# Decay products inside blocks of eight tokens as one job, and the units dealt over six jobs

## The reference, cut to what matters

```python
log_f = logaddexp(log(lb), log1p(-lb) + log_sigmoid(f_logit)); k = -expm1(log_f)
bc = cumsum(chunks(log_f), axis=3)                 # inside chunks of 64 tokens
o_inter = einsum('bhtk,bhkv->bhtv', q_ * exp(b_), state)
diff = where(causal, b_[:, :, :, None, :] - b_[:, :, None, :, :], -inf)
attn = einsum('bhtk,bhsk,bhtsk->bhts', q_, k_, exp(diff))
o_intra = einsum('bhts,bhsv->bhtv', attn, v_)
state = state * exp(b_last) + einsum('bhsk,bhsv->bhkv', k_ * exp(b_last - b_), v_)
```

## Time and profile before

| | us |
|---|---|
| median of 3 runs | 1922.56 (1920.65 to 1923.75) |
| the profiled execution | 1921.48, its span 1919.3 |
| TensorE / VectorE / ScalarE busy | 1732.6 / 864.8 / 633.9 |
| granted clock of TensorE, mean | 0.938 |

### The profile page before, as it was taken

The page is one execution under the profiler, slowest core; times in us unless marked ns, Lnnn a source line. Parts: engine busy times, 40 slices in busy tenths (PEclk is TensorE's granted clock), DMA queues, the critical chain, the costliest instruction groups (busy, mean ns, idle before and its releaser), DMA issues.

```text
span 1919.3 us, 31472 instructions
## 1 busy us (share of the span) xinstructions
PE 1732.6 (90%) x12618; PEld 1247.0 (65%) x12618; DVE 864.8 (45%) x1532; ACT 633.9 (33%) x1057; POOL 60.0 (3%) x58
## 2 busy tenths in 40 slices
PE   8999888888889899988878888999999999999997
PEld 7985334334345768543434334699988979998897
DVE  5642122121225644312212122578966556986654
ACT  4422111111114642211101111464537555443753
POOL 0100000000000010000000000100001200000110
PEclk9999889898889989988889889999989999999999
DMA  7659999999997315999999999454522334443222
GB/s 294 240 219 414 421 421 422 421 422 421 422 422 302 122 44 216 416 421 422 421 421 422 421 421 421 175 175 141 190 86 91 104 117 159 149 176 110 88 96 103
DMA packets 73095, 526.41 MB, mean 274 GB/s; under 512 B 8240, under 2 KB 8496, under 8 KB 9264
## 3 DMA queue, kind: packets, MB, share of 16 engines
q1 hardware_dynamic: 73008, 525.18, 68.7%
HBM read 524.10 MB, written 1.05 MB: 274 GB/s over the span
## 4 chain that ended last, share of the span: by engine, by line
PE 52%; DMA 28%; DVE 8%; SPq 6%; ACT 3%; issue 2%; POOL 0%; DVEq 0%; ACTq 0%
PE banks L492 13%; DMA ring<-experts 13%; DMA arena<-experts 12%; PE banks L496 10%; PE banks L498 9%; PE banks L497 9%; SPq L431 6%; PE banks L656 5%; DMA ring<-dense 3%; PE banks L638 3%; PE banks L674 3%; DVE arena L1491 1%; ACT ring_parts L1075 1%; DVE hT L1616 1%; DVE ring_parts L1471 1%
## 5 line engine op out<-in xcount | busy, mean ns | idle before, releaser
L496 PE MATMUL banks<-arena_parts,ring_parts 128*128 128x256 f32 (+1 forms) x1444 | 423.3, 293 | 17.4 <-POOL arena_parts L1404 5.8
L498 PE MATMUL banks<-arena_parts,ring_parts 128*128 128x256 f32 (+1 forms) x1444 | 412.7, 286 | 0.0
L497 PE MATMUL banks<-arena_parts,ring_parts 128*128 128x256 f32 (+1 forms) x1444 | 412.3, 286 | 0.0
L492 PEld LDWEIGHTS banks<-arena 128*128 128x128 f32 (+3 forms) x2704 | 327.7, 193 | 70.6 <-issue 54.3
L492 PE MATMUL banks<-arena 128*128 128x128 f32 (+5 forms) x2704 | 362.8, 289 | 9.2 <-ACT arena L1075 5.2
L656 PE MATMUL banks<-ring,arena 128*32 128x512 f32 x1536 | 235.2, 716 | 104.6 <-DMA ring<-experts 104.5
L1075 ACT ACTIVATE arena<-banks 128x256 f32<-128x256 f32 (+7 forms) x384 | 165.0, 457 | 424.6 <-PE banks L492 164.1
L1471 DVE TENSOR_TENSOR ring_parts<-ring,ring_parts 128x1024 fp32r<-128x1024 f32 x204 | 244.2, 1238 | 120.1 <-ACT ring_parts L1075 118.2
L496 PEld LDWEIGHTS banks<-arena_parts,ring_parts 128*128 128x128 f32 x1444 | 276.3, 191 | 31.9 <-issue 7.4
L497 PEld LDWEIGHTS banks<-arena_parts,ring_parts 128*128 128x128 f32 x1444 | 276.9, 192 | 0.1
L498 PEld LDWEIGHTS banks<-arena_parts,ring_parts 128*128 128x128 f32 x1444 | 276.3, 191 | 0.0
(11 more groups left out here) (214 smaller groups left out, 1613.5 us busy)
## 6 DMA issues: line engine op xcount, KB each, us to landing
ring<-experts SPq DMA_DIRECT2D x192, 1024.0 KB, 26.5
arena<-experts SPq DMA_DIRECT2D x160, 1024.0 KB, 22.0
ring<-dense SPq DMA_DIRECT2D x112, 1024.0 KB, 4.9
at<-experts SPq DMA_DIRECT2D x16, 1024.0 KB, 23.8
x<-experts SPq DMA_DIRECT2D x16, 1024.0 KB, 22.9
consts<-consts_in SPq DMA_DIRECT2D x1, 1414.0 KB, 13.6
vecs<-vecs_in SPq DMA_DIRECT2D x1, 1125.5 KB, 16.0
hT<-h_in SPq DMA_DIRECT2D x2, 544.0 KB, 4.5
```

The costliest lines, as they stand in the source:

```text
L492: return pe.matmul(o, lhsT, rhs, start=(k == 0), stop=(k == n - 1))
L496: pe.matmul(o, lhsT[0], rhs[0], start=(k == 0), stop=False)
L497: pe.matmul(o, lhsT[0], rhs[1], start=False, stop=False)
L498: return pe.matmul(o, lhsT[1], rhs[0], start=False, stop=(k == n - 1))
```

## The change

Spans 8, 4 and 2 and the diagonal become one job, `NEAR`, for all pairs with the key not behind the query inside blocks of eight tokens. The reference token is the fourth of the block for all of them; so both factors are made for all tokens, ScalarE makes two exps for each part (one with scale -1, straight into `b_ke` and `b_qe`), and VectorE multiplies at full width. Exponents of both signs occur now, so the floor under the logarithm, `LN_LEAST`, is raised from 2^-63 to 2^-28. The mask of the new job is the sum of the three spans' masks and the identity, made by three additions of 128x128 in the first mixture of experts. There are six jobs with products (`SPANS`), the new one first, and a seventh entry in `JOBS` without. The units and the rest are dealt over them anew; with `JOBS` the order of `MAKES`, so of the weights in memory, changes. `SPLIT_AT` is gone: one `lower_next` at each of both places in every job.

```diff
--- before.py
+++ after.py
@@ -46,7 +46,7 @@
 LEVELS = (64, 32, 16, 8, 4, 2)
 CHUNK = 64
 PAIRS = 2 * HEADS
-LN_LEAST = 2.0 ** -63
+LN_LEAST = 2.0 ** -28
 CONV_UNITS = 16
@@ -84,17 +84,20 @@
 U_HF, U_HI, U_KC, U_VC, U_KS, U_KW, U_NQ, U_VS, U_VW, U_NZ, U_HZ = 0, 8, 12, 13, 14, 15, 16, 20, 21, 22, 26
 FIRST = [("unit", u) for u in range(U_HI)]
 JOBS = [[("unit", U_HI), ("unit", U_HI + 1)],
-        [("unit", U_KC), ("unit", U_HI + 2)],
-        [("unit", U_VC), ("unit", U_HI + 3)],
-        [("unit", U_KS), ("unit", U_NQ), ("c1", 0)],
-        [("unit", U_NQ + 1), ("c1", 1), ("rot", U_KS), ("rot", U_NQ)],
-        [("unit", U_NQ + 2), ("c1sum", 0), ("c1", 2), ("rot", U_NQ + 1)],
-        [("unit", U_NQ + 3), ("unit", U_KW), ("c1", 3), ("rot", U_NQ + 2)],
-        [("unit", U_VS), ("c1sum", 1), ("rot", U_NQ + 3), ("rot", U_KW)],
+        [("unit", U_KC), ("unit", U_HI + 2), ("unit", U_HI + 3)],
+        [("unit", U_VC), ("unit", U_KS), ("c1", 0), ("unit", U_NQ)],
+        [("c1", 1), ("rot", U_KS), ("unit", U_NQ + 1), ("c1sum", 0), ("c1", 2), ("unit", U_NQ + 2)],
+        [("rot", U_NQ), ("unit", U_KW), ("c1", 3), ("rot", U_NQ + 1), ("unit", U_NQ + 3), ("c1sum", 1)],
+        [("rot", U_KW), ("unit", U_VS), ("rot", U_NQ + 2), ("rot", U_NQ + 3)],
         [("c2", 0), ("c2", 1), ("unit", U_VW), ("crot", 0)]]
 POSITIONS = {2: 0, 3: 1}
-SPLIT_AT = {0: (1, 1), 1: (1, 1), 2: (1, 1), 3: (1, 1), 4: (0, 1), 5: (0, 1), 6: (1, 1), 7: (0, 1)}
+NEAR = 8
+SPANS = (NEAR, 64, 32, 16, P, SEQ)
+MASK_OF = {64: 0, 32: 1, 16: 2, NEAR: 3, P: 6}
 BEFORE_HEADS = [("unit", U_NZ), ("unit", U_HZ)]
 IN_HEADS = [("unit", u) for u in (U_NZ + 1, U_HZ + 1, U_NZ + 2, U_HZ + 2, U_HZ + 3, U_NZ + 3)]
 GATED = {1: (0, 1), 3: (2, 3), 4: (4,), 5: (5,)}
@@ -904,24 +907,24 @@
                 for m in FIRST[6:]:
                     make(*m)
                 t.next(b2["gate_ready"])
-                for job in range(9):
+                for job in range(len(JOBS)):
                     for m in JOBS[job]:
                         make(*m)
+                    if job == len(SPANS):
+                        break
                     for part in range(2):
                         heads = range(4 * part, 4 * part + 4)
                         if job:
-                            pe.wait_ge(b2["lv_at"], 18 * layer + 2 * job - (part == 0 and job < 8))
-                        if job < 8:
-                            t.next(b2["lv_kq"])
-                        keys, queries = (b_ke, b_qe) if job < 8 else (b_k, b_p[:, F_Q:F_Q + HEADS])
+                            pe.wait_ge(b2["lv_at"], 2 * len(SPANS) * layer + 2 * job - (part == 0))
+                        t.next(b2["lv_kq"])
                         for h in heads:
-                            if job == 7:
+                            if SPANS[job] == SEQ:
                                 m = mm(flat[:, 2048 + h * P:2048 + h * P + P], b_ke[:, h, 0:P], b_qe[:, h, P:SEQ], 0, 1)
                                 continue
                             for i in range(2):
                                 at = 2048 + (2 * h + i) * P
-                                m = mm(flat[:, at:at + P], keys[:, h, i * P:i * P + P], queries[:, h, i * P:i * P + P], 0, 1)
+                                m = mm(flat[:, at:at + P], b_ke[:, h, i * P:i * P + P], b_qe[:, h, i * P:i * P + P], 0, 1)
                         m.then_inc(b2["lv_mm"], 1)
                 def scores(h):
@@ -951,7 +954,7 @@
                 scores(0)
                 tile(BEFORE_HEADS[0][1], 1, 3)
-                t.next(b2["lv_at"], 18)
+                t.next(b2["lv_at"], 2 * len(SPANS))
                 for h in range(HEADS):
                     v = [b_v[:, h // 2, i, (h % 2) * P:(h % 2) * P + P] for i in range(2)]
                     at = 2048 + h * SEQ
@@ -1312,10 +1315,14 @@
                 for m in FIRST[6:]:
                     land(*m, layer)
                 half_d = [b_d[:, part * D:part * D + D] for part in range(2)]
-                for job in range(9):
-                    if job < 8:
-                        for x in half_d:
-                            t.next(b2["lv_d"])
+                for job in range(len(JOBS)):
+                    for part, x in enumerate(half_d if job < len(SPANS) else []):
+                        t.next(b2["lv_d"])
+                        if SPANS[job] == NEAR:
+                            to_keys, to_queries = (wide(y[:, 4 * part:4 * part + 4, :]) for y in (b_ke, b_qe))
+                            act.activation(to_keys, x, ACT.Exp)
+                            act.activation(to_queries, x, ACT.Exp, scale=-1.0).then_inc(b2["lv_e"], 1)
+                        else:
                             act.activation(x, x, ACT.Exp).then_inc(b2["lv_e"], 1)
                     for m in JOBS[job]:
                         land(*m, layer)
@@ -1632,6 +1639,10 @@
                 tt(one, one, two, ALU.add)
                 tt(one, one, rep(pg, 8), ALU.mult)
                 over_groups(mo_w, one)
+                if layer == 0:
+                    lev = C("lev").rearrange("p (j t) -> p j t", j=7)
+                    for x in (lev[:, 4, :], lev[:, 5, :], C("ident")):
+                        tt(lev[:, MASK_OF[NEAR], :], lev[:, MASK_OF[NEAR], :], x, ALU.add)
                 if layer:
                     v.wait_ge(route["xr_done"], layer + 1)
                     tt(g_both[:, :], V("fing"), V("fing"), ALU.mult)
@@ -1797,15 +1808,18 @@
                 def decay(job, part):
                     b, d = wide(b_b[:, 4 * part:4 * part + 4, :]), b_d[:, part * D:part * D + D]
-                    if job < len(LEVELS):
-                        n = LEVELS[job]
+                    n = SPANS[job]
+                    if n < P:
                         x, o = (y.rearrange("p (k n) -> p k n", n=n) for y in (b, d))
+                        if n == NEAR:
+                            tt(o, x[:, :, n // 2 - 1:n // 2].to_broadcast([P, D // n, n]), x, ALU.subtract, b2["lv_d"])
+                            return
                         ref = x[:, :, n // 2 - 1:n // 2].to_broadcast([P, D // n, n // 2])
                         v.tensor_tensor(o[:, :, 0:n // 2], ref, x[:, :, 0:n // 2], ALU.subtract)
                         tt(o[:, :, n // 2:n], x[:, :, n // 2:n], ref, ALU.subtract, b2["lv_d"])
                         return
                     end = CHUNK - 1
-                    if job == 6:
+                    if n == P:
                         x, o = (y.rearrange("p (k c n) -> p k c n", c=2, n=CHUNK) for y in (b, d))
                         v.tensor_tensor(o[:, :, 0], x[:, :, 0, end:].to_broadcast([P, PAIRS // 2, CHUNK]), x[:, :, 0], ALU.subtract)
                         t.link(v.tensor_copy(o[:, :, 1], x[:, :, 1]), b2["lv_d"])
@@ -1824,11 +1838,11 @@
                         t.next(b2["at_zero"])
                     for part in range(2):
                         t.next(b2["lv_mm"])
-                        if job == 7:
+                        if SPANS[job] == SEQ:
                             at = 2048 + part * 4 * P
                             t.link(v.tensor_copy(wide(b_ax[:, 4 * part:4 * part + 4, :]), flat[:, at:at + 4 * P]), b2["lv_at"])
                             continue
-                        mask = masks[:, job, :] if job < 7 else C("ident").bitcast(U32)
+                        mask = masks[:, MASK_OF[SPANS[job]], :]
                         at = 2048 + part * D
                         t.link(v.copy_predicated(b_at[:, 8 * part:8 * part + 8, :], rep_mid(mask, 8),
                                                  flat[:, at:at + D].rearrange("p (k t) -> p k t", k=8)), b2["lv_at"])
@@ -1872,32 +1886,35 @@
                             rope(n_kc[0:32], n_crt[0:32], rep_mid(C("cosc")[0:32, :], 2), rep_mid(C("sinc")[0:32, :], 2),
                                  n_crt[0:32], b2["crope_done"])
-                for job in range(9):
-                    if job < 8:
-                        decay(job, 0)
-                        decay(job, 1)
-                        lower_next(SPLIT_AT[job][0])
+                for job in range(len(SPANS)):
+                    decay(job, 0)
+                    decay(job, 1)
+                    lower_next(1)
                     if job in POSITIONS:
                         positions(POSITIONS[job])
                     if job:
                         finish(JOBS[job - 1])
                         gather(job - 1)
-                    if job < 8:
-
-                        n = (LEVELS + (P, SEQ))[job]
-                        if job == 0:
-                            landed_by("unit", U_HI - 1)
-                        for part in range(2):
-                            t.next(b2["lv_e"])
-                            hs = slice(4 * part, 4 * part + 4)
-                            e = b_d[:, part * D:part * D + D].rearrange("p (k n) -> p k n", n=n)
-                            ke, qe, k_, q_ = (wide(x[:, hs, :]).rearrange("p (k n) -> p k n", n=n) for x in (b_ke, b_qe, b_k, q))
```

(24 more changed lines are left out.)

## The result

The changed kernel takes 1937.29 us (median of 6 runs, 1931.33 to 1940.06), the kernel before, run beside it, 1922.31 (6 runs, 1914.45 to 1926.76). The ratio is 1.0081, 95% interval 1.0064 to 1.0098: slower by 15.6 us (the two medians lie 15.0 apart). The profiled execution took 1937.06 us, its span is 1935.3, that of before 1919.3.

What follows compares the result with a forecast made beforehand. TensorE's list was taken to set the end, with VectorE's fixed order making it wait. 1921.5 + 2.3 for the stretches + 15.0 for the clock = 1938.8, rounded down to 1938 us; range 1922 to 1948.

Steps and rivals of the forecast that it cites:

- The sum's first part: In each layer's stretch: 10.5 us of removed TensorE products, 21 in all, come back as waits.
- rival A: The removed products are simply saved: 1900.5 us, or 1887 with the old waits gone as well; chance 0.09.
- The long waits: TensorE waits 3.8, 4.8 and 6.0 us in jobs 3 to 5 for units lowered behind VectorE's gather.
- The short waits: Per layer TensorE waits 1.6 us for NQ0, 0.6 for job 4's c1sum, 1.5 ahead of the compressed scores.
- TensorE's items: TensorE's work per layer, first job's products to compressed scores: 96.7 us, with 18.3 of waits 115.0.
- The clock: Dense units behind the three long waits of each layer run slow: 2.5 us per wait, 15.0 for six.
- the nearest row: Clock at 0.54 for 3.4 us after a wait of 1.88 us, costing 1.7; 1934 with that per wait.
- the upper bound: Clock loss of 3.4 us per long wait, and the waits of 1.6 and 1.5 causing one too: up to 1948.
- What was to cost nothing: Three mask additions, about 0.25 us each, in the first MoE, and VectorE's and ScalarE's longer job 0: hidden.
- B: The waits come but the clock holds, or they are 1 us shorter each: 1919 to 1926; chance 0.14.
- D: ScalarE's late landing behind a rope holds back weights, one more wait of 2 to 3 us per layer: 1944 to 1952; chance 0.15.

Runs made afterwards that it cites:

- experiment 6: Changed kernel's merged job kept, units dealt as in the kernel before with its old splits, last three lists behind the last products: 1912.19 us, ratio to before 0.9956.
- experiment 5: Kernel of experiment 4 with the half unit that followed the compressed scores made ahead of them, in another bank: 1899.02 us, ratio to before 0.9888.
- Experiment 1: Changed kernel with both VectorE lowerings of weights in jobs 3 to 5 placed ahead of gather: 1914.95 us, ratio to before 0.9963.
- experiment 2: Changed kernel with both lowerings ahead of gather in job 3 alone: 1933.87 us, ratio to before 1.0063.
- Experiment 3: Changed kernel with 4, 5 and 6 unread products of constants filling TensorE's waits ahead of NQ1, KW and VS: 1927.68 us, ratio to before 1.0032.
- experiment 4: Kernel of Experiment 1 with one unit fewer in job 2 and later ones moved one place back: 1904.25 us, ratio to before 0.9914.
- experiment 7: Kernel of experiment 5 with the near job's 16 products made twice, work only added: 1910.56 us, ratio to before 0.9941.

## Why the prediction was right

**The sum's first part.** The time of three sets of 16 products per layer was to be saved and given back. It was: the merged job alone gives 8.2 us (experiment 6) even with an uncovered end, and doubling one set costs its full 7.1 in two layers by the profile. The rival A, that the saving simply shows, missed by 37 us; its 1900.5 is about what experiment 5 reached (1899.0), once the order was mended. That the two agree so closely is partly chance: with the old waits gone as well A had 1887, and experiment 5 has waits and slow clock of its own. So the saving was there, and the step "the order lets it through" is what A lacked. On the rule of the Trainium skill ("Perfetto Trace Analysis", section "Identifying the Most-Contended Engine"): relieving the busiest engine gave +0.8% here and -1.1% with the order mended (experiment 5); the rule names the engine, and the trace's order of work decides whether its relief is seen.

**The long waits.** The working from gather's start (2.16 behind the start of the products) over the multiplications to the first half of a lowering gave 9.15 us. Job 2's products start at 1341.46, 2.06 ahead of the row of gather (1343.52), and NQ1 begins at 1350.58: 9.12. Each wait is about 0.4 shorter than predicted (3.40 for 3.8, 4.40 for 4.8, 5.56 and 5.88 for 6.0), since the products and rots that stand between took 0.2 to 0.4 longer. That VectorE's c1sum of job 4 would hold back its gather is seen in the rows above: idle for 7.94 until ScalarE's landing of a rot, then for 0.68 until ScalarE's exp of the c1sum, then gather's two halves in one go at 1394.17. The first half could have begun at about 1392.5 (the products start at 1390.43). Its end lies 6.4 behind the products' start; 6.35 was predicted. Experiment 1 shows the cause, by moving the lowerings, and experiment 2 for job 3 alone.

**The short waits.** NQ0's 1.6 was 1.46 and 1.26, the compressed scores' 1.5 was 1.05 in both layers, the c1sum's 0.6 only 0.25 and 0.16. ScalarE's part of that sum held: it had landed the c1 8.1 us behind the end of KW's unit, and 5.1 + 1.8 + 1.1 = 8.0 was summed. TensorE's items there take 7.8, so the wait of 0.6 was taken too large from the same terms. (That NQ0 takes the slot of VC follows since a c1's weights take a slot in the ring too.) In all 16.1 us of waits in place of 18.3.

**TensorE's items**: 98.2 us in place of 96.7 (119.9 less the 16.1 of waits and the 5.55 of slow clock). I took 3.49 for each job's products, from job 0; jobs 2, 3 and 4 take 3.65 to 3.75, with a c1 or a rot of another shape behind them, where job 1, with a unit behind it, takes 3.48. A rot takes 0.97, not 0.92.

**The clock.** The step was right in kind and too large in size: by the units' lengths 1.55, 1.8 and 2.2 us for the three long waits (1.5, 1.75 and 2.05 in the second layer), 10.9 in all, where 2.5 each, 15.0, was taken; the nearest row, 1.7, would have been the better value. But the wait of 1.05 ahead of the compressed scores was followed by a half unit slow by 1.5, which only the upper bound had. Experiment 3 measures the long ones of both layers, with the half units: 9.6 us. Behind the waits the mean is 0.70 to 0.77, so the clock was at its lower level for a part of each unit. The section "HAM oscillation" of the Trainium skill's page "TensorE: Matmul & The Clock Gate" tells of bursts that begin at the lower clock because of the wait ahead of each, at a penalty of half the throttled time. The trace agrees roughly: a mean of 0.77 over 7.5 us is 3.4 us at the lower level, 0.70 over 8.3 is 5.0, and the losses are 1.55 and 2.2.

**What cancelled.** By its steps the forecast had 122.5 us for each stretch, and they were 119.9 and 119.8: 5.3 us less in two layers (waits -2.2, clock -1.95, items +1.5 in each). Outside the stretches it had nothing, and there are +4.1: 1.7 ahead of the first, 1.25 between, 1.1 behind. The slow half units, 1.5 each, are enough for the last two; the 1.7 is not explained. So 1938 against 1937.3 is closer than its terms were, and that closeness is luck.

**What was to cost nothing.** The three additions take 0.95 us on VectorE in the first mixture of experts, not 0.75, and are hidden. VectorE's and ScalarE's longer job 0 is hidden too: TensorE has no wait in it.

**The other rivals.** B (waits, but the clock holds) falls by the rows of the clock and by experiment 3; with the clock's 9.6 us gone the time is 1927.7, just beyond its upper end of 1926. D did not come about in the changed kernel: ScalarE's copies of weights came in time. In the mended deal of experiments 4, 5 and 7 it did, as a wait of 1.95 to 2.13 us for ScalarE, and in experiment 1 as waits of 0.94 and 1.58.

## What to carry to other kernels

Before work is taken off the busiest engine, write down for each item behind it what it waits for, and in which place of the other engines' fixed lists that is made: work that covered a chain can be worth more than its own time. If the chain is behind a handover to the engine just relieved, move what the next item needs ahead of the handover, but only where its own inputs have landed by then. And count a wait of over 3 us ahead of dense products at more than its length: in this kernel the clock took another four tenths of it.

## What the runs showed of the hardware that was not expected

How long TensorE was idle doesn't settle whether the clock falls. A wait of 1.95 us ahead of VS was followed by a slow unit (experiment 5, in both layers), waits of 1.96 and 1.98 in the same place by units at full clock (experiment 7), and in experiment 4 one of 2.13 by a unit at full clock and one of 2.09, in the second layer, by a slow one. The plainest case stands behind the stages, in code that all nine kernels share: a wait of 1.8 to 1.9 us for GpSimd, twice in each profile. Of these eighteen, ten were followed by a slow unit (6.9 to 7.2 us) and eight by one at full clock (5.6 to 5.7 us); in experiments 2 and 5 one of each. A wait of 1.05 ahead of the small products of the compressed scores (15 columns) was followed by a slow half unit in the changed kernel and by a full clock of 1.00 in experiment 3. In experiment 7, and in the second layer of experiment 5, the clock fell to about 0.7 over 11 us where no wait was over 0.4 us, in the run of those small products. Here are the unit of experiment 5 and its clock:

```profile
1385.85 0.55 PE L500 MATMUL banks<-ring_parts,arena_parts 128*128 128x256 f32 x1 [1.95 <-ACT arena L1080]
```

```profile
1385.80:1393.20 7.40, 7.35 (x48) 7.29 (x48) 7.26 (x9) 4.89 (x7) 0.00 (x0) 0.77 0.27 112
```

Unfilled waits of 3.25 us and more were followed by slow products each time (thirteen of them: six in the changed kernel, two in experiment 1, four in experiment 2, one in experiment 6).
